# A two-block transformer kernel: the last two modulation blocks of each opening turn are multiplied on TensorE

## The reference

```python
mod = silu(c) @ w_ada + b_ada                    # c: (1, 2048), w_ada: (2048, 12288)
shift_m, scale_m, gate_m, shift_f, scale_f, gate_f = split(mod, 6)
h = rms_norm(x, pre_norm_mix) * (1 + scale_m) + shift_m
q_n, k_c, v_c, ..., v_m = split(h @ w_in, ...)   # then attention, w_o, MLP, second block
```

## Time and profile before

| | us |
|---|---|
| median of 3 runs | 2970.0 (2969.79 to 2984.42) |
| profiled execution | 2975.81 |
| its span, first to last instruction | 2974.0 |
| TensorE busy | 2884.3 |
| VectorE busy | 1661.7 |
| ScalarE busy | 1280.5 |

### The profile page before, as it was taken

One profiled execution on the slowest core, in us unless ns is written; L12 is line 12 of the kernel. 1 busy time (PEld: TensorE's weight loads), 2 busy tenths in 40 slices (PEclk: granted clock), 3 DMA queues, 4 the chain that ended last, 5 costly groups with the idle time before them and its releaser, 6 DMA issues.

```text
span 2974.0 us, 50944 instructions
## 1 busy us (share of the span) xinstructions
PE 2884.3 (97%) x22336; PEld 2659.0 (89%) x22336; DVE 1661.7 (56%) x1482; ACT 1280.5 (43%) x1210; POOL 134.0 (5%) x111
## 2 busy tenths in 40 slices
PE   6999999999999999999999999999999999999998
PEld 5999987899889997889999889999888998899887
DVE  7878877785444454455355654444745444444444
ACT  3334444444434443346344544444345443344433
POOL 0011120000000000000022320000000000000000
PEclk8799999999999999999999999999999999999999
DMA  9999778596556655545451015556554555566553
GB/s 360 387 317 307 261 246 291 180 359 219 197 186 197 192 190 184 200 165 182 159 172 62 10 45 199 188 193 226 170 186 147 191 197 186 196 192 192 183 191 120
DMA packets 300452, 596.72 MB, mean 201 GB/s; under 512 B 12144, under 2 KB 17776, under 8 KB 299760
## 3 DMA queue, kind: packets, MB, share of 16 engines
q1 hardware_dynamic: 294864, 587.83, 58.7%
q10 hardware_dynamic: 5408, 6.23, 0.8%
HBM read 583.80 MB, written 6.29 MB: 198 GB/s over the span
## 4 chain that ended last, share of the span: by engine, by line
PE 84%; DVE 8%; DMA 3%; ACT 3%; issue 2%; POOL 0%; SPq 0%; ACTq 0%; DVEq 0%
PE ps L2333 30%; PE ps L2244 26%; PE ps L2851 9%; PE ps L2436 3%; DVE ada_acc L1498 3%; PE ps L2451 3%; DVE wL L1327 2%; PE ps L2972 2%; DMA ada<-w_ada 2%; PE ps L2732 2%; PE ps L2412 1%; ACT wH L767 1%; DMA raw<-w_up 1%; PE ps L2223 0%; DMA raw<-w_in 0%
## 5 line engine op out<-in xcount | busy, mean ns | idle before, releaser
L1327 DVE TENSOR_TENSOR wL<-raw,wH 128x2048 fp32r<-128x2048 f32 x436 | 1004.6, 2304 | 1119.0 <-ACT wH L767 1114.7
L767 ACT ACTIVATE wH<-raw 128x2048 fp32r<-128x2048 f32 x436 | 837.7, 1921 | 1267.5 <-PE ps L2244 456.5
L2333 PE MATMUL ps<-actH,wH 128*128 128x256 f32 x2816 | 780.4, 277 | 6.2 <-DVE wL L1327 3.3
L2333 PE MATMUL ps<-actL,wH 128*128 128x256 f32 x2816 | 778.4, 276 | 0.0
L2333 PE MATMUL ps<-actH,wL 128*128 128x256 f32 x2816 | 778.3, 276 | 0.0
L2333 PEld LDWEIGHTS ps<-actH,wH 128*128 128x128 f32 x2816 | 529.6, 188 | 9.5 <-issue 4.7
L2333 PEld LDWEIGHTS ps<-actL,wH 128*128 128x128 f32 x2816 | 529.7, 188 | 0.1
L2333 PEld LDWEIGHTS ps<-actH,wL 128*128 128x128 f32 x2816 | 529.6, 188 | 0.0
L2244 PE MATMUL ps<-wH,hidH 128*128 128x512 f32 x1024 | 403.4, 394 | 1.3 <-DVE wL L1327 1.3
L2244 PE MATMUL ps<-wH,hidL 128*128 128x512 f32 x1024 | 400.4, 391 | 0.0
L2244 PE MATMUL ps<-wL,hidH 128*128 128x512 f32 x1024 | 397.4, 388 | 0.0
(11 more groups left out here) (429 smaller groups left out, 3650.5 us busy)
## 6 DMA issues: line engine op xcount, KB each, us to landing
raw<-w_in SPq DMA_DIRECT2D x96, 1024.0 KB, 5.2
ada<-w_ada SPq DMA_DIRECT2D x80, 1024.0 KB, 8.0
raw<-w_up SPq DMA_DIRECT2D x64, 1024.0 KB, 5.4
raw<-w_down SPq DMA_DIRECT2D x64, 1024.0 KB, 5.1
raw<-w_mlp_up SPq DMA_DIRECT2D x64, 1024.0 KB, 5.3
raw<-w_mlp_down SPq DMA_DIRECT2D x64, 1024.0 KB, 5.0
raw<-w_gates SPq DMA_DIRECT2D x48, 1024.0 KB, 5.1
raw<-w_o SPq DMA_DIRECT2D x16, 1024.0 KB, 6.5
```

What stands on the lines that cost most here:

```text
L767: nc.scalar.activation(wH[:, s % SPLIT if L[name]["spg"] > 1 else r % SPLIT, :, :], raw[:, slot, :, :], ACT.Copy).then_inc(wh_ready, 1)
L1327: nc.vector.tensor_tensor(wL[:, b, :, :], raw[:, slot, :, :], wH[:, b, :, :].bitcast(F32), ALU.subtract).then_inc(wl_ready, 1)
L2333: ins = nc.tensor.matmul(out, w[:, b, k, cols], v[:, kk, :], start=(kk == 0 and j == 0 and n % 2 == 0), stop=(kk == STEP_K * spg - 1 and j ...
```

## The change

A list `DIRECT` names blocks 6, 7, 14, 15, 22, 23, 30 and 31, the last two of each turn. VectorE no longer totals them. `ada_total` on TensorE multiplies them itself: the block is the stationary operand and the condition's column `csig` the moving one, 16 matmuls of one column for each block, added in PSUM to the group's total. `summed(j)` counts the `ada_sum` increments of the blocks before j without the direct ones, and replaces the former counts in all waits. A modulation block that takes the slot of a direct one waits for `ada_rows` instead of `ada_sum`.

TensorE's totals both stand behind the third step. Behind total 1 it issues six fp32 matmuls of 256 columns that nobody reads. SP's order of weight and modulation blocks is new, and so are the places of the splits, coefficients and low halves in VectorE's loop.

```diff
+    DIRECT = (6, 7, 14, 15, 22, 23, 30, 31)
+        def summed(j):
+            return STEP_K * (j - sum(n < j for n in DIRECT))
@@ SP
             def ada_block(j):
-                if ada_before[j] >= 0:
-                    sp.wait_ge(ada_sum, STEP_K * (ada_before[j] + 1))
+                if ada_before[j] in DIRECT:
+                    sp.wait_ge(ada_rows, ada_before[j] // 4 + 1)
+                elif ada_before[j] >= 0:
+                    sp.wait_ge(ada_sum, summed(ada_before[j] + 1))
...
-            for j in range(1, 4):
+            for j in range(1, 8):
                 ada_block(j)
-            for c in range(KT // STEP_K):
+            for c in range(KT // STEP_K - 1):
+                after = {0: 1, 1: 2} if c == 0 else {1: 1, 2: 2}
+                if c == 0:
+                    weight_block(0)
                 for n in range(8):
-                    if 8 * c + n + 4 < NFRONT:
-                        ada_block(8 * c + n + 4)
-                    if c == 0 and n >= 5:
-                        weight_block(n - 5)
-                    if c in (1, 2) and n in (2, 5, 7):
-                        weight_block(FRONT * c + n // 3)
-                    if c == 3 and n == 2:
-                        weight_block(FRONT * c)
+                    if c < 2 and n == 7:
+                        weight_block(FRONT * (c + 1))
+                    ada_block(8 * (c + 1) + n)
+                    if n in after:
+                        weight_block(FRONT * c + after[n])
+            weight_block(FRONT * 3)
             weight_block(FRONT * 3 + 1)
...
             weight_block(FRONT * 3 + 2)
             sp.dma_start(c1[:, :], a["c1"]).then_inc(c1_in, 16)
+            ada_block(NFRONT)
             weight_block(FRONT * 3 + 3)
+            ada_block(NFRONT + 1)
+            sp.wait_ge(ada_sum, summed(NFRONT))
+            sp.wait_ge(ada_rows, NFRONT // 4)
+            sp.dma_start(posk[:, :, :], a["pos"]).then_inc(pos_in, 16)
             weight_block(9 + RAW)
-            ada_block(NFRONT)
-            ada_block(NFRONT + 1)
-            sp.wait_ge(ada_sum, STEP_K * NFRONT)
-            sp.dma_start(posk[:, :, :], a["pos"]).then_inc(pos_in, 16)
...
@@ VectorE: total() and ada_block() take a function "beside", called behind a block's second instruction
             for c in range(KT // STEP_K):
-                for n in range(8):
+                if c == 1:
+                    front_coefficients(0)
+                    front_split(0, 0)
+                    front_low(0)
+                    front_split(0, 1)
+                if c > 1:
+                    front_split(c - 1, 0)
+                for n in range(6):
+                    if c > 1 and n == 1:
+                        front_coefficients(c - 1)
+                        ada_block(8 * c + n, lambda: front_low(c - 1))
+                        front_split(c - 1, 1)
+                        continue
                     ada_block(8 * c + n)
-                    if c == 0 and n == 6:
-                        over_root(0)
-                    if c and n == (c > 1):
-                        front_coefficients(c - 1)
-                        front_split(c - 1, 0)
-                        front_low(c - 1)
-                    if c and n == (c > 1) + 1:
-                        front_split(c - 1, 1)
-                    if c and n == (c > 1) + 2:
+                    if c and n == 2:
                         front_split(c - 1, 2)
-                    if c and n == 5:
+                    if n == 5:
                         over_root(c)
+            front_coefficients(3)
             front_split(3, 0)
-            front_coefficients(3)
@@ TensorE
             def ada_total(g, bank, col):
+                last = 4 * g + 3
+                direct = [j for j in range(4 * g, 4 * g + 4) if j in DIRECT]
+                for j in direct:
+                    pe.wait_ge(ada_in[ada_slot[j]], ada_count[j])
+                    for n in range(GT):
+                        for k in range(STEP_K):
+                            r = j % 4 * STEP_K + k
+                            nc.tensor.matmul(ps[:, bank, col + n:col + n + 1], adas[ada_slot[j]][:, k, n * P:(n + 1) * P],
+                                             csig[:, r:r + 1], start=(j == direct[0] and n == 0 and k == 0), stop=False,
+                                             skip_group_check=True)
...
+            def unread(n, bank):
+                for _ in range(n):
+                    nc.tensor.matmul(ps[:, bank, P:P + T], ident, common[:, 0:T], start=True, stop=True)
             front_total(0)
             front_total(1)
+            unread(6, 4)
...
-                    if c < 3 and n == 1:
-                        front_total(2 * c + 2)
                 if c < 3:
+                    front_total(2 * c + 2)
                     front_total(2 * c + 3)
```

More of the change, by code:

```diff
@@ L603, in _ @@
             sp.dma_start(c1[:, :], a["c1"]).then_inc(c1_in, 16)
+            ada_block(NFRONT)
             weight_block(FRONT * 3 + 3)
+            ada_block(NFRONT + 1)
+            sp.wait_ge(ada_sum, summed(NFRONT))
+            sp.wait_ge(ada_rows, NFRONT // 4)
+            sp.dma_start(posk[:, :, :], a["pos"]).then_inc(pos_in, 16)
             weight_block(9 + RAW)
-            ada_block(NFRONT)
-            ada_block(NFRONT + 1)
-            sp.wait_ge(ada_sum, STEP_K * NFRONT)
-            sp.dma_start(posk[:, :, :], a["pos"]).then_inc(pos_in, 16)
             weight_block(10 + RAW)
             sp.dma_start(cw1[:, 0, :, :], a["cmp_k_w1"].rearrange("(l d) h -> d l h", d=P)).then_inc(cmp_in, 16)
+            weight_block(11 + RAW)
             sp.dma_start(cw1[:, 1, :, :], a["cmp_v_w1"].rearrange("(l d) h -> d l h", d=P)).then_inc(cmp_in, 16)
@@ L614, in _ @@
             sp.dma_start(cw2[:, 1, :], a["cmp_v_w2"]).then_inc(cmp_in, 16)
-            weight_block(11 + RAW)
             used = NFRONT
@@ L628, in _ @@
                                 ada_block(n)
-            sp.wait_ge(ada_sum, STEP_K * (NFRONT + NWIN))
+            sp.wait_ge(ada_sum, summed(NFRONT + NWIN))
             for r in range(L["w_o"]["groups"]):
@@ L656, in ring_free @@
                         elif s < UP_ADA[r] and L.block(name, r, s) + 1 == j - RAW:
-                            sp.wait_ge(ada_sum, STEP_K * (up_ada(r, s)[2] + 1))
+                            sp.wait_ge(ada_sum, summed(up_ada(r, s)[2] + 1))
             def flat_stream(name):
@@ L690, in _ @@
                 stream(name)
-            sp.wait_ge(ada_sum, STEP_K * 6 * KT)
+            sp.wait_ge(ada_sum, summed(24 * STEP_K))
             sp.dma_start(c2[:, :], a["c2"]).then_inc(c2_in, 16)
@@ L944, in w_in_out @@
                 if r == 6:
-                    act.wait_ge(ada_sum, STEP_K * (NFRONT + 30))
+                    act.wait_ge(ada_sum, summed(NFRONT + 30))
                 nc.scalar.activation(flat(proj[:, tile_of(r):tile_of(r) + GT, :]), bank2(0), ACT.Copy).then_inc(evacuated, 1)
@@ L951, in v_tokens @@
                 if n == 2:
-                    act.wait_ge(ada_sum, STEP_K * (NFRONT + 24))
+                    act.wait_ge(ada_sum, summed(NFRONT + 24))
                 dst = vtokN[:, 2 * n:2 * n + 2, :, :] if n < 2 else vtokM[:, 2 * n - 4:2 * n - 2, :, :]
@@ L1483, in token_inputs, with total @@
                         split(name, 0, 0, 1)
-            def total(j, w):
+            def total(j, w, beside=None):
                 g = j // 4
@@ L1495, in total @@
                     else:
-                        dve.wait_ge(ada_sum, 4 * STEP_K * g + n - 1)
+                        dve.wait_ge(ada_sum, summed(4 * g) + n - 1)
                         ins = nc.vector.scalar_tensor_tensor(sums[:, n % 2, :], w[:, k, :], csig[:, n:n + 1], sums[:, n % 2, :],
@@ L1500, in total, with ada_block @@
                     ins.then_inc(ada_sum, 1)
+                    if beside and k == 1:
+                        beside()
                 if j % 4 == 3 and g >= 8:
-                    dve.wait_ge(ada_sum, 4 * STEP_K * (g + 1))
+                    dve.wait_ge(ada_sum, summed(j + 1))
                     nc.vector.tensor_tensor(sums[:, 0, :], sums[:, 0, :], sums[:, 1, :], ALU.add).then_inc(ada_merged, 1)
-            def ada_block(j):
+            def ada_block(j, beside=None):
                 dve.wait_ge(ada_in[ada_slot[j]], ada_count[j])
-                total(j, adas[ada_slot[j]])
+                total(j, adas[ada_slot[j]], beside)
             def modulation(g, bank):
@@ L2366, in ada_total @@
             def ada_total(g, bank, col):
+                last = 4 * g + 3
[8 more added lines that the diff above has]
+                                             skip_group_check=True)
                 if g < 8:
-                    pe.wait_ge(ada_sum, 4 * STEP_K * (g + 1))
+                    pe.wait_ge(ada_sum, summed(last + 1))
                 else:
@@ L2377, in ada_total @@
                         ins = nc.tensor.matmul(ps[:, bank, col + n:col + n + 1], ada_sums(g)[:, j, n * P:(n + 1) * P],
```

(3 more changed lines are left out.)

## The result

| | before | after |
|---|---|---|
| median, same session | 2973.9 us (4 runs) | 3017.4 us (4 runs) |
| ratio, 95% interval | | 1.0129 (1.0108 to 1.0149) |
| profiled execution, span | 2974.0 us | 3016.3 us |
| last front step ends | 161.1 us | 197.4 us |
| mean granted clock | 0.981 | 0.971 |

The change makes the kernel slower by 1.3%. A second session gave 3012.3 against 2975.1, ratio 1.0137 (1.0121 to 1.0153). The forecast was +32 us; the medians moved by 44 us in the first session and by 37 in the second, and both times, 3017 and 3012, lie above the range that ended at 3011.

A forecast was written before the change was run, and what follows sets the result against it. VectorE and transfers bound the opening before; the change makes TensorE the bound. Opening +33, 1 us given back, net +32: profiled 2975.8 to 3008 us, or 3002 against the 2970.0 median; range 2970 to 3011.

The forecast's parts named there:

- Which level: Direct stream on TensorE: 2.4 GHz for 4.5 us from the third step's end, then 1.2 GHz.
- Rival A: Opening: clock stays at 2.4 GHz in the direct stream, last coefficients at 137.6, time 2966 us; chance 0.20.
- The tail, 17.3 us: From a turn's third step to the coefficients: 4.5 us at full clock, then 58 records taking 12.8 us.
- The steps, 17.93: A turn's three TensorE steps take 17.93 us, with the slow start they had in the last turn.
- First total and slots: Opening's first turns: coefficients at 49, then 92; slot waits put the third split at 67.5, making the third step wait 2 us.
- Sum: Opening: coefficients at 49, 92, 132.4 and 172.8, last front step at 195.9 against 161.1; taken as +33 us.
- a second pace, 193: Same opening sum with 0.214 us a record, the slow gate part's pace: last front step at 193.
- Given back, 1 us: Stage at 138 to 200 us, freer of transfers: at most 2 us come back, 1 taken.
- the forecast's own +22 to +41: Whole kernel: the main forecast's own range, 2992 to 3011 us, at chance 0.60.
- The new order of the weight blocks and the moved splits spare no path then: each is early.: Opening, with TensorE as the bound: reordered weight blocks and moved splits gain nothing.

The follow-up runs named there:

- the wide operand: Changed kernel with the direct matmuls' moving operand 112 columns wide, 111 of them zeros, instead of 1: 2987.1 us, ratio 1.0038.
- the second profile: Profile of the changed kernel run once more, unedited, for the spread of its runs: 3012.3 us.

## Why the prediction was wrong

Its mechanism was right and its size too small: a turn with its tail was 41.3 us, not 40.4, the sum was then taken 2 us below its own working, and the clock of a later stage was priced at nothing. By its steps:

*Which level.* Right: the clock fell in each tail and stayed at 0.50 until some 3.3 to 3.9 us into the next wide matmuls, and the wide operand shows it to be the cause. The Trainium skill's sentence on activity ("TensorE: Matmul & The Clock Gate", Part 1: The HAM clock gate), read as busy time, fails here: TensorE was 100% busy at 0.50. Rival A's clock came about only with wide matmuls.

*The tail, 17.3 us: near by luck.* Measured 17.6, 17.8 and 17.9 (74.08 to 91.70, 115.20 to 132.98, 156.30 to 174.20). Two misses cancel in it. I gave the higher clock 4.5 us; it lasted 2.5 to 2.8, and 3.1 to 3.4 in the second profile. I took 0.12 and 0.22 us a record from totals that stood alone; in the stream they are 0.105 (1.68/16) and 0.213 (3.41/16). With these paces and my 4.5 us the 96 records would come to 15.8 us, by estimate, so the earlier fall cost 2 us a tail. The tail before held 3.03 us in which TensorE waited for VectorE, not for the transfers, as I wrote.

*The steps, 17.93.* Measured 18.1 to 18.4, and 18.6 to 18.9 in the second profile: the rise of the clock came later into the first step than in the earlier trace rows.

*First total and slots.* Coefficients at 49 and 92 forecast, 48.5 and 91.7 measured; the third split at 67.5 forecast, its end at 66.9 measured. The transfers ran dry as said (share 0 from 56 to 60 us) and lay inside TensorE's time.

*Sum: the term that was mis-sized.* Working from the rows gave a last front step at 195.9. I then took a second pace, 193, and settled on +33. Measured 197.4, +36.3. The second pace, 0.214 a record, was the one that the trace shows, but with it alone my rows give 194.4, not 193, and it left the 4.5 us at full clock in, which were too long. The other 1.5 us above 195.9 are the turns of 41.3 us.

*Given back, 1 us.* In the first profile nothing came back by the end of `w_in` (+36.4 at the start of the next stage, +37.3 there); in the second 1.3 us did (36.7 and 35.4) and were gone again at the end (+37.0).

*Behind it* no step of mine had anything. The first profile lost 7.0 us in the last recurrence turn at the low clock (35.0 late ahead of that stretch, 42.0 behind it); the second lost 0.2 there and ended 37 late. By their mean clocks two more runs of the first session are like the first profile. So of the 10 us that the first profile is above the forecast's +32, some 3 are the opening and most of the rest is that turn. The range's own upper end allowed 1.5 us a turn of the opening, and nothing for the later stages, though the three runs shown before already differed by 15. The second session's +37 lies inside the forecast's own +22 to +41; the first session's +44 does not.

*"The new order of the weight blocks and the moved splits spare no path then: each is early."* True in the changed kernel only because TensorE hid it. With VectorE in the lead the new loop costs 8 us of the opening (170.2 against 162.2). I had priced the loop under one bound only.

The parts do not add up, since each hides another: direct stream at 1.2 GHz against 2.4, 29.3 us (197.4 to 168.1); two direct blocks against none at 2.4 GHz in the new loop, -2.1 (168.1 against 170.2), in the old one +1.5 (163.7 against 162.2), and 7 to 10 in the whole time (2981 against 2974, from two sessions).

## What to carry to other kernels

Before moving reductions to TensorE as matmuls of one or a few columns, look for a stretch of such matmuls in the profile and read its granted clock: here the stream ran at half speed, and with it the gate part and the start of the next dense work. If they must stay, try the moving operand padded with zeros: at 2.4 GHz a record of 112 columns took 0.113 us (7.24/64) and one of a single column 0.105, so the 111 more columns cost little, and with the clock kept they made the stream 5.4 us shorter. And price an edit under the bound that will be there after the other parts, and once more without them.

## What was not expected of the hardware

One 256-column fp32r matmul behind each one-column fp32 matmul (two records) did not hold the clock (0.54 over 19 us); 112 columns in every matmul did (1.00 over 10 us). A stage of small matmuls 1600 us later ran at 0.60 or 0.94 of the clock in two profiles of one program, which cost 7 us; such a stage moves single profiles of this kernel by as much as several of the edits here. In the same program the clock fell 2.5 to 2.8 us into the narrow matmuls of a tail in one profile and 3.1 to 3.4 in another.
